# Two norms taken from one pass of sums between two blocks, with pooling pieces moved apart and a bias band laid out on the host

## The reference, cut to what matters

```python
def rms_norm(x, g):
    y = x * lax.rsqrt(jnp.mean(x * x, axis=-1, keepdims=True) + EPS)
    return y * g

# first block
h = x + stick_breaking_mixer(rms_norm(x, norm_mix), sb_w_qkv, sb_w_o)
h = h + sq_relu_mlp(rms_norm(h, norm_mlp), mlp_w1, mlp_w2)
x = rms_norm(h, final_norm)                       # factor r3
# second block
z = rms_norm(x, pre_mix_g) @ w_in                 # factor r4; z = q, k, v, u
a = chunked_attention(q, k, v, rel_bias)          # softmax over a band with a bias by distance
p = multiscale_pool(u, pool_w, pool_scale)        # trailing means over 2, 4, 8, 16 tokens, less the token
x = x + rms_norm(concat(a, p) @ w_o, post_mix_g)
up = causal_dwconv(rms_norm(x, pre_ffn_g) @ w_up, conv_w, conv_b)   # factor r6
x = x + rms_norm((gelu(up[:, :F]) * up[:, F:]) @ w_down, post_ffn_g)
```

## Time and profile before

| what | value |
|---|---|
| time before, median of 3 runs | 2181.11 us (2180.69 to 2185.06) |
| the profiled execution's own time | 2181.66 us |
| its span, from first to last instruction | 2179.9 us |
| busy: PE, PEld | 2141.5 us (98%), 1852.9 us (85%) |
| busy: DVE, ACT, POOL | 1288.1 us (59%), 1063.2 us (49%), 237.5 us (11%) |
| mean granted TensorE clock | 0.995 of full speed |
| weights and inputs read | 395.55 MB, 182 GB/s over the span |

### The profile page before, as it was taken

How to read it: one execution, slowest core, us unless ns; L and a number is a source line. 1 busy time by engine, 2 the same in 40 slices (tenths; PEclk the granted TensorE clock), 3 DMA queues, 4 the chain that set the end, 5 groups by cost and what they waited for, 6 DMA issues and landing times. The chain is left out here.

```text
span 2179.9 us, 28147 instructions
## 1 busy us (share of the span) xinstructions
PE 2141.5 (98%) x11706; PEld 1852.9 (85%) x11706; DVE 1288.1 (59%) x1331; ACT 1063.2 (49%) x1186; POOL 237.5 (11%) x137
## 2 busy tenths in 40 slices
PE   7999999999999999999998999999999999999998
PEld 6888888888888888888887888888888888888886
DVE  7455556655555555556677755566666644566655
ACT  5554554544434443444444545455555433555553
POOL 2000000100000000000025000032222100222211
PEclk9999999999999999999999999999999999999999
DMA  7445555565555655565564555635555656556553
GB/s 254 165 145 194 168 169 188 170 205 181 201 188 183 199 186 187 175 209 192 190 197 136 184 176 175 195 115 188 185 185 193 210 194 190 178 175 202 193 195 115
DMA packets 208289, 399.49 MB, mean 183 GB/s; under 512 B 12321, under 2 KB 16545, under 8 KB 208033
## 3 DMA queue, kind: packets, MB, share of 16 engines
q1 hardware_dynamic: 206976, 395.60, 55.5%
q10 hardware_dynamic: 1184, 2.10, 0.3%
HBM read 395.55 MB, written 2.10 MB: 182 GB/s over the span
## 5 line engine op out<-in xcount | busy, mean ns | idle before, releaser
L951 DVE TENSOR_TENSOR Wl<-raw,Wh 128x1024 fp32r<-128x1024 f32 x746 | 920.2, 1253 | 639.3 <-ACT Wh L755 639.3
L1234 PE MATMUL ps<-aHL,Wh 128*128 128x512 f32 x3328 | 1171.3, 397 | 16.7 <-DVE Wl L951 14.8
L755 ACT ACTIVATE Wh<-raw 128x1024 fp32r<-128x1024 f32 x746 | 769.9, 1054 | 617.7 <-PE ps L1234 615.1
L1234 PE MATMUL ps<-aHL,Wl 128*128 128x256 f32 x3328 | 931.6, 280 | 0.0
L1234 PEld LDWEIGHTS ps<-aHL,Wh 128*128 128x128 f32 x3328 | 627.7, 189 | 164.5 <-issue 18.6
L1234 PEld LDWEIGHTS ps<-aHL,Wl 128*128 128x128 f32 x3328 | 630.8, 190 | 0.6 <-issue 0.2
L1234 PE MATMUL ps<-hid,Wh 128*128 128x512 f32 x1024 | 355.1, 391 | 0.0
L1234 PE MATMUL ps<-hid,Wl 128*128 128x256 f32 x1024 | 286.7, 280 | 0.0
L1234 PEld LDWEIGHTS ps<-hid,Wh 128*128 128x128 f32 x1024 | 191.5, 187 | 42.0
L1234 PE MATMUL ps<-Wh,hid 128*128 128x512 f32 x704 | 217.6, 389 | 0.0
L1234 PEld LDWEIGHTS ps<-hid,Wl 128*128 128x128 f32 x1024 | 193.5, 189 | 0.0
(11 more groups left out here) (159 smaller groups left out, 1288.2 us busy)
## 6 DMA issues: line engine op xcount, KB each, us to landing
raw<-in_mlp_w_dram SPq DMA_DIRECT2D x256, 512.0 KB, 4.3
raw<-in_w_up_dram SPq DMA_DIRECT2D x176, 512.0 KB, 3.7
raw<-in_sb_w_qkv_dram SPq DMA_DIRECT2D x96, 512.0 KB, 4.5
raw<-in_w_down_dram SPq DMA_DIRECT2D x88, 512.0 KB, 4.1
raw<-in_w_in_dram SPq DMA_DIRECT2D x64, 512.0 KB, 4.4
raw<-in_sb_w_o_dram SPq DMA_DIRECT2D x32, 512.0 KB, 4.5
raw<-in_w_o_dram SPq DMA_DIRECT2D x32, 512.0 KB, 3.9
xT<-in_x_dram SPq DMA_DIRECT2D x4, 512.0 KB, 7.5
```

Of the source, the lines that this page charges most:

```text
L755: e.activation(Wh[:, i % NW, :], rawv[:, i % NRAW, :], ACT.Copy).then_inc(st["hi"][0], 1)
L951: e.tensor_tensor(Wl[:, i % NW, :], rawv[:, i % NRAW, :], Wh[:, i % NW, :].bitcast(F32), ALU.subtract).then_inc(st["lo"][0], 1)
L1234: return e.matmul(o, l, r, start=start, stop=stop, skip_group_check=True)
```

## The change

It has six parts.

- **Both norms from one pass.** While the last MLP's residual tiles are finished, ACT squares them twice: as before, and once more with the gain `final_norm` as a scale (`gained_squares`, 16 instructions on one tile each). POOL sums both. One step, `rms_pair` at u0 + 5, makes r3 from the first sums, and r4 from the second sums times r3 squared. `spread_pair` at u0 + 6 turns both into rows. The squares of the normed `xT` go, and `norm_x` moves to u0 + 8 to u0 + 11.
- **Pooling.** `windows` is put down with its strip's sum, at u0 + 7 and u0 + 15. `means` stands at u0 + 12 and u0 + 22. The second pooling piece moves behind the k strip, to u0 + 33, while the first stays at u0 + 24.
- **Bias.** The host writes the band out as it is needed, and one DMA of the same 1 MB fills `vb`. The flip, its products, the copy back and POOL's flipped identity go. The cut by a memset stays, at u0 + 7.
- **r6 later.** Its `rms` moves on by two pieces (i + 8 to i + 10), and the first conv strip's scaling with it (`later(2)` to `later(4)`).
- **Stick breaking.** `halves` stands three pieces behind the scores instead of two.
- **Space.** `rs` grows to 40 columns, and the second diagonal `D2` lies behind `D`.

```diff
+    def gained_squares(n, need):
+
+        sq, half = done("gsq_squared", 4), done("gsq_halved")
+        quart = done("gsq_quartered") if n else None
+        total = done("gsq_total")
+        step("gained_squares", n=n, need=need, free=free["qk0"] + free["qk1"], zs_free=list(free["zs"]), sq=sq, half=half,
+             quart=quart, total=total, before=st.get("gained_total") if n else None)
+        st["gained_total"] = total
...
+    def rms_pair():
+
+        s = side_set()
+        total, mean = done("rms_total"), done("rms_mean", 2)
+        first = dict(root=done("rms_root"), rec=done("rms_rec"), sq=done("rms_rec"), prod=done("rms_rec"), r=done("rms_r"))
+        square, moved, mean2 = done("rms_moved"), done("rms_moved"), done("rms_mean")
+        second = dict(root=done("rms_root"), rec=done("rms_rec"), sq=done("rms_rec"), prod=done("rms_rec"), r=done("rms_r"))
+        both = done("rms_r")
+        diag = done("rms_diag", 2)
+        step("rms_pair", set=s, need=[st["total"], st["gained_total"]], free=list(free[f"set{s}"]), ones=ones0, ident=ident,
+             total=total, mean=mean, first=first, square=square, moved=moved, mean2=mean2, second=second, both=both, diag=diag)
+        free["zs"], free[f"set{s}"] = [total], [mean]
+        st["r3c"], st["r4c"] = first["r"], both
+
+        def spread_pair():
+            s = side_set()
+            turned, copied = done("row_turned"), done("row_copied", 2)
+            step("spread_pair", set=s, diag=diag, free=list(free[f"set{s}"]), turned=turned, copied=copied)
+            free[f"set{s}"], free["zs"] = [copied], [turned]
+            free["qk0"], free["qk1"] = [st["gained_total"]], [st["gained_total"]]
+            st["r3"], st["r4"] = copied, copied
+        after(p.at + 1, spread_pair, ahead=True)
...
                 st["sp", g] = lo
-            later(2, halves)
+            later(3, halves)
...
                 later(0 if s4 == 3 else 1, lambda: squares(s4, ("xT", s4), [high]))
+                if gain_name == "in2":
+                    later(0 if s4 == 3 else 1, lambda: gained_squares(s4, [high]))
...
     def load_bias(s, k):
-        loaded, zero, flip = done("bias", 16), done("flip_zero"), done("flip_set")
-        step("load_bias", need=k, loaded=loaded, zero=zero, flip=flip)
-        st["bias0"], st["flip"] = loaded, flip
-
-    def turn_bias():
-        s = side_set()
-        mm, copied, cut = done("bias_mm"), done("bias_copied"), done("bias_cut")
-        step("turn_bias", set=s, need=[st["bias0"], st["flip"], *free[f"set{s}"]], mm=mm, copied=copied, cut=cut)
-        free[f"set{s}"] = [copied]
+        loaded, cut = done("bias", 16), done("bias_cut")
+        step("load_bias", need=k, loaded=loaded)
+
+        def cut_bias():
+            step("cut_bias", loaded=loaded, cut=cut)
+        later(8, cut_bias)
         st["bias"] = cut
...
         def f():
             d = done("x_normed", 4)
             step("norm_x", q=q, need=[st["r3"], *tile_hl[4 * q:4 * q + 4]], done=d)
-            later(1, lambda: squares(q, ("xT", q), [d], odd="mT"))
...
                 free["T0"], free["T1"], free["E"] = last, last, last
-                later(2 if u == 0 else 5, lambda: means(last))
+                later(5 if u == 0 else 7, lambda: means(last))
...
                 free["T0"], free["T1"], free["E"] = ([h[1][1]] for _ in range(3))
-            later(5 if u == 0 else 0, windows)
+            windows()
...
     u0 = strip("w_in_2", 3072, ALL8, "aHL", tile_hl, evac_pool(0))
     strip("w_in_2", 3072 + STRIP, ALL8, "aHL", tile_hl, evac_pool(1))
+    def pool_piece(j):
+        p.pieces.append(dict(src=("pool_w_2", "groups", 2 * j, 0), shape=4, mov="oHL2", kt=4 * j, tiles=pool_tiles,
+                             kind="P", first=True, last=True, evac=evac_mix(j)))
+
     for g in range(2):
         first2["q", g] = strip("w_in_2", g * STRIP, ALL8, "aHL", tile_hl, evac_qk(0, g, QSCALE, "r_b", "r4"))
         if g == 0:
-            for j in range(2):
-                p.pieces.append(dict(src=("pool_w_2", "groups", 2 * j, 0), shape=4, mov="oHL2", kt=4 * j, tiles=pool_tiles,
-                                     kind="P", first=True, last=True, evac=evac_mix(j)))
+            pool_piece(0)
         first2["k", g] = strip("w_in_2", 1024 + g * STRIP, ALL8, "aHL", tile_hl, evac_qk(1, g, 1.0, "r_b", "r4"))
+        if g == 0:
+            pool_piece(1)
         first2["v", g] = strip("w_in_2", 2048 + g * STRIP, ALL8, "aHL", tile_hl, evac_v(g, 2), kind="N")
     first2["o"] = len(p.pieces)
-    after(u0 + 3, r_job("r3", "a", "r_a"))
+    after(u0 + 5, rms_pair)
     for j in range(4):
-        after(u0 + 5 + j, norm_x(j))
-    after(u0 + 11, r_job("r4", "b", "r_b", "a"))
-    after(first2["q", 0] + 5, turn_bias)
...
-            later(0 if "r6" in st else 2, scaled)
+            later(0 if "r6" in st else 4, scaled)
...
                 if at + j + which == 0:
-                    after(i + 8, r_job("r6", "b", "r_b"))
+                    after(i + 10, r_job("r6", "b", "r_b"))
...
-        rs = sb("rs", [128, 24])
+        rs = sb("rs", [128, 40])
...
-        D = zs[:, 512:512 + TOK]
+        D, D2 = zs[:, 512:512 + TOK], zs[:, 768:768 + TOK]
...
+                elif k == "gained_squares":
+                    n = st["n"]
+                    for t in st["need"] + st["free"]:
+                        e.wait_ge(*t)
+                    for j in range(4 * n, 4 * n + 4):
+                        e.activation(mT[:, j, :], xT[:, j, :], ACT.Square, scale=G["final"][:, j:j + 1]).then_inc(st["sq"][0], 1)
...
+                elif k == "rms_pair":
+                    e.wait_ge(*st["mean"])
+                    mean, r, y, h = moments(slice(0, 2))
+                    e.activation(r, mean, ACT.Sqrt).then_inc(st["first"]["root"][0], 1)
+                    e.wait_ge(*st["mean2"])
+                    mean, r, y, h = moments(slice(0, 2), 24)
+                    e.activation(r, mean, ACT.Sqrt).then_inc(st["second"]["root"][0], 1)
+                elif k == "spread_pair":
+                    e.wait_ge(*st["turned"])
+                    for n, r in ((1, r_a), (2, r_b)):
+                        e.activation(r[:, :], ps[st["set"]][:, n, 0:TOK], ACT.Copy).then_inc(st["copied"][0], 1)
...
                     e.wait_ge(*st["need"])
-                    e.dma_start(Bt[:, :, :], src).then_inc(st["loaded"][0], 16)
-                elif k == "turn_bias":
-                    e.wait_ge(*st["mm"])
-                    e.activation(vb2[:, :], ps[st["set"]][:, :, :].rearrange("p b n -> p (b n)"),
-                                 ACT.Copy).then_inc(st["copied"][0], 1)
+                    e.dma_start(vb2[:, :], A["rel_band"]).then_inc(st["loaded"][0], 16)
...
+                elif k == "rms_pair":
+                    a, b = cols["a"], cols["b"]
+                    mean, gained, r3_sq = rs[:, 0:2], rs[:, 32:34], rs[:, 34:36]
+                    mean2 = moments(slice(0, 2), 24)[0]
+                    e.wait_ge(*st["total"])
+                    e.tensor_scalar(mean, ps[st["set"]][:, 0, 0:2], 1.0 / 2048, EPS, ALU.mult, ALU.add).then_inc(st["mean"][0], 1)
+                    e.tensor_scalar(gained, ps[st["set"]][:, 0, 2:4], 1.0 / 2048, None, ALU.mult).then_inc(st["mean"][0], 1)
+                    newton(st["first"], a, slice(0, 2), st["first"]["sq"])
+                    e.wait_ge(*st["first"]["r"])
+                    e.tensor_tensor(r3_sq, a, a, ALU.mult).then_inc(st["square"][0], 1)
+                    e.wait_ge(*st["square"])
+                    e.wait_ge(*st["mean"])
+                    e.tensor_tensor(gained, gained, r3_sq, ALU.mult).then_inc(st["moved"][0], 1)
+                    e.wait_ge(*st["moved"])
+                    e.tensor_scalar(mean2, gained, EPS, None, ALU.add).then_inc(st["mean2"][0], 1)
+                    newton(st["second"], b, slice(0, 2), st["second"]["sq"], 24)
+                    e.wait_ge(*st["second"]["r"])
+                    e.tensor_tensor(b, b, a, ALU.mult).then_inc(st["both"][0], 1)
+                    diagonal(a, st["first"]["r"], st)
+                    diagonal(b, st["both"], st, D2)
...
-                elif k == "turn_bias":
-                    e.wait_ge(*st["copied"])
+                elif k == "cut_bias":
+                    e.wait_ge(*st["loaded"])
                     e.memset(Bt[0:64, :, 192:256], -1e30).then_inc(st["cut"][0], 1)
...
+                elif k == "gained_squares":
+                    n = st["n"]
+                    B = mT[:, 4 * n:4 * n + 4, :]
+                    e.wait_ge(*st["sq"])
+                    e.tensor_tensor(B[:, 0:2, :], B[:, 0:2, :], B[:, 2:4, :], ALU.add).then_inc(st["half"][0], 1)
+                    e.wait_ge(*st["half"])
+                    if n == 0:
+                        for t in st["zs_free"]:
+                            e.wait_ge(*t)
+                        e.tensor_tensor(Z4[:, 1, :], B[:, 0, :], B[:, 1, :], ALU.add).then_inc(st["total"][0], 1)
+                    else:
```

(82 more changed lines are left out.)

10 lines of the change are left out of this document (4 added, 6 removed).

## The result

The changed kernel took 2198.49 us (median of 4 runs, 2198.30 to 2198.94), the kernel before 2183.09 us beside it (4 runs, 2180.69 to 2186.08): 1.0066 times as long, 95% interval 1.0053 to 1.0080. Forecast were 2169 us. The profiled execution took 2198.94 us.

A forecast was written before the change was run, and what follows sets the result against it. PE was taken as the bound: products of 746 pieces plus its waits. Wins of 21.8 us less costs of 9.4 gave 12.4 us off the profiled 2181.66, so 2169 us, range 2160 to 2176.

The forecast's parts named there:

- DVE and POOL excluding each other: Rival from u0 + 8 to u0 + 27: DVE cannot catch up, PE waits; 2183 to 2188 us, chance 0.04.
- (1): Between the blocks: PE's wait for POOL's r4 sum goes, with the low clock behind it; wins 8.1 us.
- (2): At r6: PE's 3.45 us wait for a DVE sum goes, with 2.7 us of clock; wins 6.1 us.
- (3): Flip of the bias: its products on PE go, the band's DMA stays hidden; wins 3.0 us.
- (4): Around the pooling pieces: idle time for ACT's bias copy and two sums goes; wins 2.5 us.
- (5): Stick breaking in the first block's attention: four of five PE waits go; wins 2.1 us.
- (6): Pair of norms: PE waits before the turning for a chain of some 3.7 us; costs 1.1 us.
- (7): Strip u0 + 8: DVE's splits and norm run late beside POOL's windows, PE waits; costs 1.5 us (0 to 3.3).
- (8): k strip: PE waits 4.0 us for the q strip's set, plus 2.8 us of low clock; costs 6.8 us.

The follow-up runs named there:

- e2: Changed kernel with rs back at 24 columns and its 16 new columns in a buffer behind all others (shift 0): 2164.40 us, 0.9920.
- e7: e2 with the r6 part undone (sums at i + 8, scaling two pieces on): 2170.63 us, 0.9948.
- e8: e2 with the stick-breaking part undone (halves two pieces behind the scores): 2167.49 us, 0.9930.
- e12: e2 with both pooling pieces behind the k strip, the first directly in front of the second: 2159.64 us, 0.9894.
- e4: Changed kernel with rs at 88 columns, so buffers behind it start 256 bytes later than in the kernel before: 2165.38 us.
- e9: e2 with the first pooling piece moved behind the k strip and the second behind the v strip: 2168.83 us, 0.9936.
- e14: e2 with the edits of e12 and e13 together: 2157.94 us, 0.9886.
- e13: e2 with aHL alone moved 32 bytes, oHL1, hid1 and what follows by 256: 2162.38 us, 0.9907.
- e11: Changed kernel with rs at 96 columns, a shift of 288 bytes against the kernel before: 2171.49 us.
- e6: Kernel before with 64 unused bytes put in just ahead of aHL, behind the weights and rs: 2212.72 us, 1.0134.
- e1: Kernel before with rs of 40 instead of 24 columns, nothing else: 2211.40 us, 1.0133.
- e10: Changed kernel with rs at 72 columns, a shift of 192 bytes against the kernel before: 2192.08 us.

## Why the prediction was wrong

**The step that failed** stands in its first part: "the time is the products of 746 pieces plus what PE waits, and a change can win only PE's waits, extra PE work, or PE's clock". The products' own duration was taken as fixed (2.77 us per piece), and so the part "Space" has no term in the sum at all. What it did: 2016 single products at 6.5 ns more are 13.1 us. Of 4624 pairs, 1920 with `aHL` in the first block and the q, k and pooling strips take 5.9 ns more, 1408 with `aHL` in the convolution strips 3.4 (part of them was slow already), 1024 with `hid` 6.6 and 272 with `oHL` 6.3, by the pitches of e2 and the changed kernel: 24.6 us. Together 37.7 us. The k strip gives 2.7 us of it back (2.2 us without the low clock against e2's 4.9), so 35.0. Measured: 2198.49 - 2164.40 = 34.1 us. No rival had this mechanism either. The slower side was given to DVE and POOL excluding each other, which did not come.

**The rest, by its numbers**, read at shift 0 (e2), where nothing else is mixed in. The forecast for it was 2169; it took 2164.4. Product by product, e2's profiled execution ends 18.1 us ahead of that of the kernel before: 3.2 us come in the first block, 8.8 between the blocks and 6.1 at r6. The prediction's terms for these places are 2.1, 4.2 (13.6 less 9.4) and 6.1.

- (1) The r4 wait, 8.1 us: gone, with the low clock behind it. Right. It was not undone alone.
- (2) r6, 6.1 us: gone, and 6.1 us is what e2 gains there on the kernel before. Back in e7 it cost 5.1, with the same 3.45 us of waiting and 1.7 instead of 2.7 of clock. Nothing new was late behind it. Right.
- (3), (4) The flip and the waits at the pooling pieces, 5.5 us: gone from the trace. Right; not tried alone.
- (5) Stick breaking, 2.1 us: four waits back in e8, 2.1 us, as forecast. The step was worth more, 3.2 us against the kernel before and 3.6 against e8, since the pairs behind each wait were slow too; this the sum left out. ACT still stands, 2.18 instead of 3.13 us, but one more split is ahead of it. Timeline of ACT in the changed kernel:

```profile
159.52 1.49 ACT L839 ACTIVATE E_hi<-E 128x1536 fp32r<-128x1536 f32 x1 [2.18 <-POOL E L1209]
```

- (6) The pair's chain, 1.1 us: 0.9 us, which is what its own 3.7 - 2.77 gives. Right.
- (7) DVE in the strip u0 + 8, 1.5 us (0 to 3.3): no wait at all, the lower bound. The step was right in its kind and too dear. The four norm instructions beside POOL took 6.21 us, more than the worst row had (3.67), but only those met POOL; the other twelve took 1.66 us for four. By the exclusive lock of the Trainium skill ("SBUF — State Buffer", "Who interferes with whom") such stretches are to be expected; the trace agrees, and shows that it is one group, not all sixteen instructions.
- (8) The k strip, 6.8 us: 4.9 us in e2, and e12 wins 4.8 at this place by removing the wait. The mechanism was right, the wait (4.0) was 3.16 and the clock (2.8) 1.7. That the low clock came at all was not certain: in e4 it did not, behind a wait as long. I had taken PE there at 1188.6; in e2 its last product before the wait ends at 1184.8, and in the changed kernel, with its slower products, at 1206.6.

Steps (6) to (8) came to 5.8 instead of 9.4 us. That is 3.6 of the 5.7 us by which the gain of the profiled execution (18.1) exceeds the forecast (12.4), and step (5) is 1.1. The last 1.0 us lies between the blocks and is not placed.

**What stays open.** Why the distance counts is not shown. PE reads both operands of a product from SBUF, one as the weight load and one as the moving side, and a conflict between the two reads would fit a period of 256 bytes, but no run looked into it. Nor did one tell it from a conflict of PE's reads with another engine that uses the weights' buffers at the same time. By the Trainium skill ("SBUF — State Buffer", "Who interferes with whom") these two reads of PE have ports of their own and are independent; the pitches here show that they are not free of each other's place, or that something else depends on it. Why pairs with `aHL` or `oHL` fall to the slow pitch in some stretches at shift 0 and 256, and not at 32, is open too; at the same layout e8 and e2 differ behind the waits, and e9 and e2 in a whole pass. If the pitch of a pass changed from one execution to the next, it would fit that the four times of e4 spread over 6.4 us and those of e14 over 0.4, but with one trace per program this is not shown. Whether other distances than the six tried are still better is open as well.

## What to carry to other kernels

In a kernel bound by PE, compare the mean duration of one product in a stretch that the change does not touch, before looking at any wait: 21 products fewer in 200 us at full clock gave the cause away. A buffer that grows by some columns moves all buffers behind it; put new scratch at the end, or pad to 256 bytes, and treat the layout as a part of the change with a price. Where a wait stands between two strips that alternate two sets, moving a one-piece strip can remove it (e12) or put a longer one elsewhere (e9), since each piece moved also changes which set all the following strips take. Set two traces of nearly the same program against each other product by product: this told the price of a place from what the rest of the execution did, where the medians could not (e9, e12).

## What the runs showed of the hardware

- The pitch of products with rounded fp32 operands depends on the place of the activations against the weights in SBUF. The places tried fit a period of 256 bytes: 0 and 256 gave the same pitches with `hid`, and 32 (e13) and 288 (e11) gave `aHL`'s single products the same slow one. The pitch is 346.7 or 353.3 ns for a pair, 226.8 or 233.3 ns for a single product, with values between at 128 (both) and 192 bytes (single products). It cost up to 1.6% of this kernel's time. Granted clock, DMA share and idle time do not show it: 1.00, 0.58 and none in both windows.
- The two forms of product ask for different places. A shift of 32 bytes is fast for pairs (activations first) and slow for single products (weights first), 0 is fast for both, 64 slow for both. Pairs with `aHL` in the convolution strips are an exception: at 0 and at 64 one shift gave two pitches in the same pass (346.7 in e2 and 353.3 in e9; 353.3 in e6 and 348.9 in e1), and at 256 both passes were slow (e4).
- In these traces the length of PE's idle stretch does not by itself tell whether the lower clock follows. 3.16 us (e2) was followed by a mean clock of 0.64 over 4.7 us, 3.15 us (e4) by 1.00. 2.24 us (e8) and 2.29 us (e10) were followed by 0.64, 2.21 us (changed kernel) and 2.23 us (e7) by 1.00.
